# Two transformer layers in one kernel: the delta rule's norms as chains of their own, the second attention on five-unit steps, the merge as a list of pairs

## The chip, the cores and the metric

The kernel runs on one core of a Trainium2 chip. The metric is device time in microseconds for one execution of the whole program. It has five engines with an instruction queue each: PE (matrix multiplications; weight loads are listed as PEld), DVE (vector), ACT (activations and copies), POOL and SP. Each queue is worked off in its written order, and an instruction that waits for a semaphore holds up everything behind it on its engine. All the tensors are float32, and a sequence of 256 tokens with 2048 channels passes through.

## The reference, cut to what matters

Two layers follow each other. The first has a projection, an indexed attention, a state-space part and an MLP. The second is this:

```python
def hybrid_layer_2(x, ...):
    h = rms_norm(x, ln1_w)
    nsa_q, nsa_kv, nsa_gate, gdn_qkv, gdn_z, gdn_a, gdn_b, merge = split(h @ w_in)
    o_a = nsa_attention(nsa_q, nsa_kv, nsa_gate, rel_table, ...)      # 8 heads, three branches
    o_b = gated_deltanet(gdn_qkv, gdn_z, gdn_a, gdn_b, ...)           # 8 heads
    g_a, g_b = split(sigmoid(merge))
    x = x + (g_a * (o_a @ w_pa) + g_b * (o_b @ w_pb)) @ w_o
    h = rms_norm(x, ln2_w)
    return x + square(relu(h @ w_up)) @ w_down

def gated_deltanet(...):
    qkv = silu(causal_depthwise_conv(qkv, conv_w))
    q, k, v = split(qkv)
    q = q * rsqrt(sum(q * q) + eps) * 128 ** -0.5                     # norm of q
    k = k * rsqrt(sum(k * k) + eps)                                   # norm of k
    o = chunked delta rule(q, k, v, g, beta)                          # chunks of 64 tokens
    o = o * rsqrt(mean(o * o) + eps) * norm_w                         # norm of the output
    return o * silu(z)
```

The relative bias of `nsa_attention` comes from a table of 32 buckets for 8 heads, spread over 512 distances. The first layer's indexed attention scores each of 256 keys for two blocks of 128 queries; the first block may look at the first 128 keys alone.

## The kernel before, in words

**Weights.** Every weight matrix streams through a ring of four 1 MB pieces. A piece is two *units* of 128x1024. ACT copies a unit, rounded, to `w_hi` (L1778), DVE puts the rest in `w_lo` (L1049), and PE multiplies a unit in 16 instructions, eight with `w_hi` and 512 columns and eight with `w_lo` and 256 columns (L450, L453). Four units can be ready ahead of PE. Results leave the three GEMM banks in halves: ACT lifts one half (L1784), and DVE adds the other (L1069).

**Rounds.** The order on each engine is written by generators. `drain(a, b, c)` takes one step of each in turn until all are done; such a turn is a *round* here. In the last place stands the generator of the projections, which gives one weight unit a round; the ones before it are chains of small work which PE, DVE and ACT hand to each other, put between units so that their waits are covered. The same rounds are written for each engine.

**The second layer's stages around the change**, in units: `gdn0` and `gz0` (32, first half of the delta rule's projections) run beside the attention, two chains `nsa(0)` and `nsa(1)` of eight iterations that are four rounds long, both chains in the same round. In an iteration PE makes the logits (L875), DVE and ACT the softmax (L1586 to L1597, L2214), PE turns the probabilities (L883), ACT and DVE copy them (L2219, L1600), PE multiplies them with the values (L896). Then come the 32 units of `gdn1` and `gz1` and the 48 of `merge(0)` (gates and projections of `w_pa`), beside the delta rule: two chains, one after another for the heads' two halves, with 42 rounds a half. Six of the 86 rounds hold no unit. A half begins with the norms of q and k, in four rounds: ACT squares (L2245), PE sums with a matrix of ones (L917), ACT takes the root (L2248), DVE the reciprocal and the product (L1629, L1631); then follow decays and products of keys (L927 to L936), a matrix inverse in five levels for each of two token blocks (L942, L950, L955; DVE L1661 to L1667) and four chunks. It ends with the norm of the output (PE L1005, ACT L2280, DVE L1706 to L1715), whose result, multiplied with silu(z), is what `w_pb` is multiplied with. Then follow the 48 units of `merge(1)` alone, and `w_o`, whose input needs the merged sum converted in two parts, eight pairs on ACT (L2326) and on DVE (L1747).

**First layer.** Beside the projections of q, k and v, PE makes the bias table with eight matmuls of one head each (L571) and the sixteen score matmuls of 512 columns (L584: two heads by 256 keys).

A merge step of the kernel before is a fixed sequence of six units, gate first:

```python
for s in range(KD // 2):
    gate, proj = gate_bufs[m][s % len(gate_bufs[m])], pair(merged, s) if m == 0 else proj_bufs[s % 2]
    for i in range(6):        # units 0 to 3: two gate tiles; 4 and 5: two tiles of w_pa or w_pb
```

## Time and profile before

| what | us |
|---|---|
| time, median of 3 runs (2809.63 to 2811.53) | 2811.52 |
| time of the profiled execution | 2812.39 |
| its span, first to last instruction | 2810.4 |
| PE busy in it | 2713.7 |
| DVE busy | 1824.5 |
| ACT busy | 1375.7 |

A busy PE is one with a matmul under way. The profile lists how long each engine was busy, what its idle time waited for, and which share of TensorE's clock was granted: 1.00 is 2.4 GHz and 0.50 is 1.2 GHz. The span and what lies around it differ by 2.0 us, so what is saved in the span is saved in the time.

### The profile page before, as it was taken

To read this page: it belongs to the slowest core of one execution; us is meant where nothing else is said; L and a number is where in the kernel's file an instruction comes from. 1 tells how busy PE (TensorE), PEld (TensorE's weight loads), DVE (VectorE), ACT (ScalarE), POOL (GpSimd) and SP (SyncE) were. 2 spreads that over 40 slices of the span, in tenths; PEclk is the share of its full clock that TensorE was granted. 3 is DMA by queue.
4 is the path that set the end of the run, shared out by engine and by line. 5 is a ranking of instruction groups with operands and counts; after the bars stand their busy time and mean duration, and the time that the engine had idled before them with its cause. 6 is when DMAs were issued, how large, how long until landed. Compare 5 with 4: busy or idle time off the path is not lost. (4 is left out here: it accounts for less than half of the span.)

```text
span 2810.4 us, 38297 instructions
## 1 busy us (share of the span) xinstructions
PE 2713.7 (97%) x15590; PEld 2346.5 (83%) x15590; DVE 1824.5 (65%) x2514; ACT 1375.7 (49%) x1938; POOL 200.2 (7%) x174
## 2 busy tenths in 40 slices
PE   7999999999999999999998989999999999999998
PEld 6678888888888888888777869978888888888887
DVE  6686697655656556685658776566666556566565
ACT  5646545535445345465654444444445344454443
POOL 3004101000000000130312200000000000000001
PEclk9999999999999999999999999999999999999999
DMA  6444445555555555565333314355455555555553
GB/s 241 149 166 142 160 147 183 193 187 184 199 181 185 199 186 195 210 222 201 120 113 112 122 60 138 119 193 191 169 180 182 195 193 189 183 196 185 182 199 110
DMA packets 66711, 482.07 MB, mean 172 GB/s; under 512 B 7431, under 2 KB 7559, under 8 KB 9576
## 3 DMA queue, kind: packets, MB, share of 16 engines
q1 hardware_dynamic: 65232, 468.74, 47.9%
q0 software_dynamic: 928, 9.70, 0.9%
q8 instruction: 124, 2.03, 0.3%
q10 hardware_dynamic: 376, 1.17, 0.1%
q14 instruction: 51, 0.42, 0.0%
HBM read 473.30 MB, written 6.29 MB: 171 GB/s over the span
## 5 line engine op out<-in xcount | busy, mean ns | idle before, releaser
L1049 DVE TENSOR_TENSOR w_lo<-weight_ring,w_hi 128x1024 fp32r<-128x1024 f32 x886 | 1081.6, 1231 | 622.2 <-ACT w_hi L1778 614.5
L1778 ACT CAST w_hi<-weight_ring 128x1024 fp32r<-128x1024 f32 x886 | 917.7, 1048 | 658.7 <-PE bank L453 631.9
L450 PE MATMUL bank<-mix,w_hi 128*128 128x512 f32 x3840 | 1226.0, 401 | 8.5 <-DVE mix L1747 4.3
L450 PE MATMUL bank<-h,w_hi 128*128 128x512 f32 x2864 | 912.8, 400 | 9.3 <-DVE w_lo L1049 9.3
L453 PEld LDWEIGHTS bank<-mix,w_lo 128*128 128x128 f32 x3840 | 727.1, 189 | 172.5
L453 PE MATMUL bank<-mix,w_lo 128*128 128x256 f32 x3840 | 759.7, 279 | 0.0
L453 PEld LDWEIGHTS bank<-h,w_lo 128*128 128x128 f32 x2864 | 538.9, 188 | 127.4
L450 PEld LDWEIGHTS bank<-mix,w_hi 128*128 128x128 f32 x3840 | 590.8, 190 | 14.7 <-issue 7.7
L453 PE MATMUL bank<-h,w_lo 128*128 128x256 f32 x2864 | 563.8, 278 | 0.0
L450 PEld LDWEIGHTS bank<-h,w_hi 128*128 128x128 f32 x2864 | 439.2, 189 | 24.2 <-issue 22.6
L1784 ACT COPY arena<-bank 128x256 f32<-128x256 f32 x283 | 104.8, 372 | 383.5 <-PE bank L453 367.6
L1069 DVE TENSOR_TENSOR arena<-arena,bank 128x256 f32<-128x256 f32 x281 | 117.3, 419 | 147.0 <-ACT arena L1784 146.5
L2346 POOL TENSOR_TENSOR arena<-arena 128x512 f32<-128x512 f32 x30 | 47.2, 1574 | 1812.5 <-ACT arena L1846 1812.1
L1118 DVE TENSOR_TENSOR arena<-arena,bank 128x256 f32<-128x256 f32 x176 | 74.0, 421 | 68.1 <-PE bank L453 67.9
L2072 ACT ACTIVATE arena<-arena 128x512 f32<-128x512 f32 x64 | 40.5, 632 | 85.2 <-DVE arena L1415 85.2
L1121 DVE TENSOR_TENSOR arena<-arena,bank 128x256 f32<-128x256 f32 x176 | 74.2, 421 | 6.0
L1423 DVE TENSOR_TENSOR mix<-arena,mix 128x512 fp32r<-128x512 f32 x64 | 43.9, 686 | 10.8 <-ACT mix L2074 10.8
L1415 DVE SCALAR_TENSOR_TENSOR arena<-arena 128x512 f32<-128x512 f32 x64 | 44.3, 692 | 6.9 <-DVE arena L1069 0.5
L2362 POOL TENSOR_SCALAR arena<-arena,vecs 128x256 f32<-128x256 f32 x24 | 26.0, 1084 | 284.7 <-DVE arena L1069 244.7
L2363 POOL TENSOR_SCALAR arena<-arena,vecs 128x255 f32<-128x255 f32 x36 | 42.1, 1169 | 0.0
L2262 ACT COPY arena<-bank 128x256 f32<-128x256 f32 x40 | 14.6, 373 | 54.8 <-PE bank L950 53.6
L2074 ACT CAST mix<-arena 128x512 fp32r<-128x512 f32 x64 | 39.7, 620 | 2.0
(340 smaller groups left out, 1688.5 us busy)
## 6 DMA issues: line engine op xcount, KB each, us to landing
weight_ring<-in_w_up SPq DMA_DIRECT2D x128, 1024.0 KB, 4.9
weight_ring<-in_w_down SPq DMA_DIRECT2D x128, 1024.0 KB, 4.8
weight_ring<-in_w_merge SPq DMA_DIRECT2D x32, 1024.0 KB, 4.9
weight_ring<-in_w_gdn SPq DMA_DIRECT2D x24, 1024.0 KB, 4.9
weight_ring<-in_w_papb SPq DMA_DIRECT2D x16, 1024.0 KB, 4.8
weight_ring<-in_w_o SPq DMA_DIRECT2D x16, 1024.0 KB, 4.9
weight_ring<-in_w_xbc SPq DMA_DIRECT2D x12, 1024.0 KB, 4.9
weight_ring<-in_w_q SPq DMA_DIRECT2D x8, 1024.0 KB, 4.8
```

Source lines behind the costliest of these rows:

```text
L450: e.matmul(bank[:, :], w_hi[:, unit_at % UNITS, o + j * P:o + (j + 1) * P], x[:, :, at + j * S:at + (j + 1) * S], start=first and j == 0, ...
L453: done = e.matmul(bank[:, 0:S], w_lo[:, unit_at % UNITS, o + j * P:o + (j + 1) * P], x[:, 0, at + j * S:at + (j + 1) * S], start=False, st ...
L1049: e.tensor_tensor(w_lo[:, i, :], ring[:, p % PIECES, half * UNIT:(half + 1) * UNIT], w_hi[:, i, :].bitcast(F32), ALU.subtract).then_inc(un ...
L1069: e.tensor_tensor(dst, dst, bank[:, 0:S], ALU.add).then_inc(read, 1)
L1118: e.tensor_tensor(tile(xT, t), tile(xT, t), bank[:, 0:S], ALU.add).then_inc(res_half, 1)
L1121: e.tensor_tensor(tile(xT, t), tile(xT, t), bank[:, S:2 * S], ALU.add).then_inc(read, 1)
L1415: e.scalar_tensor_tensor(out=split(buf, 2), in0=split(buf, 2), scalar=0.0, in1=over(root_m, 2), op0=ALU.max, op1=ALU.mult).then_inc(up_sca ...
L1423: e.tensor_tensor(pair(hid[:, 1, :], n % 8), relu_m[n % 3], pair(hid[:, 0, :], n % 8).bitcast(F32), ALU.subtract).then_inc(up_lo, 1)
L1778: e.copy(w_hi[:, i, :], ring[:, p % PIECES, half * UNIT:(half + 1) * UNIT]).then_inc(unit_hi, 1)
L1784: e.copy(dst, psum[use % 3][0:dst.shape[0], S:2 * S]).then_inc(lifted, 1)
L2346: e.tensor_tensor(sq_total, sq_total, sq_bufs[s % 2], ALU.add).then_inc(res_gathered, 1)
L2363: e.tensor_scalar(tmp[:, 1:S], src[:, 0:S - 1], vec(name, 2 * tiles + t), None, ALU.mult).then_inc(conv_near, 1)
```

## The change

- The norms of q and k leave `delta_rule`. `unit_vectors(half)` is a chain of its own with four norms, one after another: for the first half it runs beside the attention from round 22 on, for the second beside the first half's delta rule from round 21 on. The sum goes to bank 7, square and root to free space in `h` (`h_plain`).
- The output's norm becomes `delta_out(half, c)`. For the first half it runs together with the second half's `delta_rule`, and the two chains are two rounds apart.
- `nsa` takes five rounds an iteration where it took four, and chain 1 begins two rounds after chain 0. DVE gives up its turn between the maximum and the reciprocal.
- The merge is a list of pairs of tiles, `gate` (four units) or `proj` (two). Three gates go beside the attention (12 units), 15 pairs (44 units) beside the delta rule, 14 (40 units) behind it. The six empty rounds are gone. The merged sum is converted from the pair `proj 1, 6` on, and one pair of eight is left for after the merge.
- First layer: one bias matmul of eight columns of output for all heads, written out to the same DRAM table by a broadcasting DMA; the eight score matmuls of the first query block take 256 columns and not 512.

```diff
@@ order of the merge
+MERGE_EARLY = [("gate", 0, 0), ("gate", 0, 1), ("gate", 0, 2)]
+MERGE_BEFORE = [("gate", 0, 3), ("gate", 0, 4), ("proj", 0, 0), ("proj", 0, 1), ("proj", 0, 2), ("gate", 0, 5),
...
+                ("proj", 0, 7), ("gate", 1, 0), ("gate", 1, 1)]
+MERGE_BEHIND = [item for s in range(6) for item in (("proj", 1, s), ("gate", 1, s + 2))] + [("proj", 1, 6), ("proj", 1, 7)]
@@ PE, first layer
-                for hd in range(NSA_HEADS):
-                    if hd > 0:
-                        e.wait_ge(rows_copied, hd)
-                    e.matmul(psum[7][:, :], rel[:, hd:hd + 1].to_broadcast([REL_BUCKETS + 1, P]), hot, start=True,
-                             stop=True).then_inc(rows_summed, 1)
-                    yield from rounds(2)
+                e.matmul(psum[7][0:NSA_HEADS, :], rel, hot, start=True, stop=True).then_inc(rows_summed, 1)
...
-                    e.matmul(psum[3 + n % 2][:, :], tile(qiT, t)[:, qb * P:(qb + 1) * P], kiT, start=True,
-                             stop=True).then_inc(score_dotted, 1)
+                    nk = P * (qb + 1)
+                    e.matmul(split(psum[3 + n % 2][:, :], 2)[:, :, 0:nk], tile(qiT, t)[:, qb * P:(qb + 1) * P],
+                             split(kiT, 2)[:, :, 0:nk], start=True, stop=True).then_inc(score_dotted, 1)
@@ PE, attention
+                yield from rounds(2 * c)
...
-                    yield from rounds(2)
+                    yield from rounds(3)
@@ PE, norms
+            def unit_vectors(half):
+                for n in range(4 * half, 4 * half + 4):
+                    yield
+                    e.wait_ge(unit_squared, n + 1)
...
+                    e.matmul(psum[7][:, :], ones[:, :], unit_sq[n % 2], start=True, stop=True).then_inc(unit_summed, 1)
+                    yield
...
+            def delta_out(half, c):
+                yield from rounds(2 * c + 1)
...
+                e.matmul(psum[7][:, :], ones[:, :], tail_bufs[c][0], start=True, stop=True).then_inc(tail_pe[c], 1)
+                yield
...
+            def delta_chain(c):
+                return one_after_another(delta_rule(0, c), together(delta_out(0, c), delta_rule(1, c)), delta_out(1, c))
@@ DVE, norms
+            def unit_vectors(half):
+                for n in range(4 * half, 4 * half + 4):
+                    root = unit_root[n % 2]
+                    yield from rounds(2)
+                    e.wait_ge(unit_rooted, n + 1)
+                    e.reciprocal(root, root).then_inc(unit_inv, 1)
...
@@ every engine, the two drains
-            drain(one_after_another(compressed(), together(nsa(0), nsa(1))), gdn_projections(0))
+            drain(one_after_another(compressed(), together(nsa(0), nsa(1))),
+                  one_after_another(rounds(22), unit_vectors(0)),
+                  one_after_another(gdn_projections(0), merge(MERGE_EARLY)))
...
-            drain(one_after_another(delta_rule(0, 0), delta_rule(1, 0)),
-                  one_after_another(delta_rule(0, 1), delta_rule(1, 1)),
-                  one_after_another(gdn_projections(1), rounds(6), merge(0)))
-            drain(merge(1))
+            drain(delta_chain(0), delta_chain(1), one_after_another(rounds(21), unit_vectors(1)),
+                  one_after_another(gdn_projections(1), merge(MERGE_BEFORE)))
+            drain(merge(MERGE_BEHIND))
```

How the instructions stand now at two places. The first is DVE's queue where the first half of the delta rule gives way to the second. Before: the end of chain 1's output norm (L1706 to L1715), then the first two norms of the second half (L1629, L1631) with a unit's `w_lo` (L1049) and bank halves (L1069) between them.

```order
L1706 RECIPROCAL arena<-arena 128x512
L1708 SCALAR_TENSOR_TENSOR arena<-arena,vecs 128x512
L1712 TENSOR_TENSOR arena<-arena 128x512
L1715 TENSOR_TENSOR h<-arena,h 128x512
L1049 TENSOR_TENSOR w_lo<-weight_ring,w_hi 128x1024 x2
L1069 TENSOR_TENSOR arena<-arena,bank1 128x256
L1049 TENSOR_TENSOR w_lo<-weight_ring,w_hi 128x1024
L1069 TENSOR_TENSOR arena<-arena,bank2 128x256
L1629 RECIPROCAL arena<-arena 128x512
L1631 SCALAR_TENSOR_TENSOR arena<-arena 128x512
L1629 RECIPROCAL arena<-arena 128x512
L1631 SCALAR_TENSOR_TENSOR arena<-arena 128x512
```

Now, in the second half's rounds 3 to 5: L1780 to L1775 are the level steps (L1666, L1667, L1661 before), L1826 to L1832 chain 1's output norm, L1125 and L1145 the unit's `w_lo` and bank half.

```order
L1125 TENSOR_TENSOR w_lo<-weight_ring,w_hi 128x1024
L1780 TENSOR_TENSOR arena<-arena,bank3 128x256
L1781 TENSOR_TENSOR arena<-arena,bank3 128x256
L1775 TENSOR_TENSOR arena<-arena,const_mats 128x256
L1826 RECIPROCAL arena<-arena 128x512
L1828 SCALAR_TENSOR_TENSOR arena<-arena,vecs 128x512
L1832 TENSOR_TENSOR arena<-arena 128x512
L1780 TENSOR_TENSOR arena<-arena,bank5 128x256
L1781 TENSOR_TENSOR arena<-arena,bank5 128x256
L1775 TENSOR_TENSOR arena<-arena,const_mats 128x256
L1125 TENSOR_TENSOR w_lo<-weight_ring,w_hi 128x1024
L1145 TENSOR_TENSOR arena<-arena,bank0 128x256
```

The output norm moved from before the second half into its levels, and it stands between the level steps of chain 0 and of chain 1.

The second place is ACT's queue in the attention. Before: L2214 is the softmax of both chains at once (four instructions), L1992 the convolution's silu, L2219 the copies of turned probabilities.

```order
L1784 COPY arena<-bank0 128x256
L1992 ACT_TABLE_LOAD
L1992 ACTIVATE arena<-arena 128x256
L2214 ACT_TABLE_LOAD
L2214 ACTIVATE arena<-arena 128x128 x4
L1778 CAST w_hi<-weight_ring 128x1024 x2
L1784 COPY arena<-bank1 128x256
L1992 ACT_TABLE_LOAD
L1992 ACTIVATE arena<-arena 128x256
L2219 COPY arena<-bank3 128x256
L2219 COPY arena<-bank5 128x256
```

Now the same stage: L2312 is one chain's softmax, L2089 the silu, L2317 and L2321 copies of one chain.

```order
L2089 ACT_TABLE_LOAD
L2089 ACTIVATE arena<-arena 128x256
L2321 CAST h<-bank3 128x128
L1876 CAST w_hi<-weight_ring 128x1024
L2312 ACT_TABLE_LOAD
L2312 ACTIVATE arena<-arena 128x128 x2
L2317 COPY arena<-bank6 128x256
L1876 CAST w_hi<-weight_ring 128x1024
L1882 COPY arena<-bank1 128x256
L2089 ACT_TABLE_LOAD
L2089 ACTIVATE arena<-arena 128x256
```

The chains' exponentials stand apart now, with a table load each. In the whole program ACT's queue has 66 table loads before and 89 now, 17 and 30 of them in the attention's stage.

## Rows read from the trace of the kernel before

**Rows 1.** The page, part 1: busy us (share of the span) and instructions.
```profile
PE 2713.7 (97%) x15590; PEld 2346.5 (83%) x15590; DVE 1824.5 (65%) x2514; ACT 1375.7 (49%) x1938; POOL 200.2 (7%) x174
```
**Rows 2.** Waits of PE, 1310 to 2000 us: total us, times, longest us.
```profile
PE bank L917 <- ACT arena L2245: 13.5, 4, 7.0
PE bank L883 <- DVE arena L1597: 7.7, 8, 1.4
PE bank L450 <- DVE w_lo L1049: 6.6, 1, 6.6
PE bank L935 <- DVE arena L1631: 4.8, 3, 1.9
PE bank L450 <- DVE mix L1747: 4.3, 1, 4.3
PE bank L896 <- DVE arena L1600: 3.9, 6, 0.8
PE bank L942 <- DVE arena L1655: 3.4, 2, 2.3
PE bank L896 <- ACT arena L2219: 2.7, 1, 2.7
```
**Rows 3.** Waits of PE, 1640 to 1686 us alone.
```profile
PE bank L917 <- ACT arena L2245: 11.2, 3, 7.0
PE bank L935 <- DVE arena L1631: 1.4, 1, 1.4
```
**Rows 4.** Windows: length, busy us PE, PEld, DVE, ACT, POOL; PEclk, DMA, GB/s.
```profile
1320.00:1476.00 156.00, 141.70 (x797) 119.84 (x796) 99.92 (x201) 92.01 (x185) 36.32 (x36) 0.96 0.33 113
1476.00:1508.00 32.00, 24.19 (x133) 19.91 (x132) 30.25 (x37) 14.23 (x23) 8.04 (x8) 0.95 0.19 63
1651.00:1686.00 35.00, 28.16 (x133) 21.61 (x134) 30.22 (x34) 18.67 (x28) 0.00 (x0) 0.86 0.26 91
1845.00:1850.00 5.00, 4.80 (x18) 4.17 (x19) 3.49 (x6) 4.30 (x7) 0.00 (x0) 0.65 0.92 324
1987.00:1994.00 7.00, 6.23 (x26) 5.42 (x27) 5.23 (x10) 3.08 (x5) 0.00 (x0) 0.76 0.46 152
2200.00:2240.00 40.00, 40.00 (x232) 34.89 (x231) 23.80 (x30) 15.26 (x15) 0.00 (x0) 1.00 0.54 187
```
**Rows 5.** Groups of PE, 60 to 200 us: busy us, mean ns, idle before.
```profile
L584 PE MATMUL bank<-arena 128*128 128x512 f32 x32 | 16.4, 595 | 1.4 <-DVE arena L1178 1.4
L571 PE MATMUL bank<-arena 33*128 33x512 f32 x16 | 9.0, 641 | 0.0
```
**Rows 6.** Groups of DVE, 1300 to 1880 us.
```profile
L1049 DVE TENSOR_TENSOR w_lo<-weight_ring,w_hi 128x1024 fp32r<-128x1024 f32 x130 | 158.0, 1225 | 81.8 <-ACT w_hi L1778 81.2
...
L1629 DVE RECIPROCAL arena<-arena 128x512 f32<-128x512 f32 x8 | 26.8, 3348 | 5.2 <-ACT arena L2248 5.2
...
L1667 DVE TENSOR_TENSOR arena<-arena,bank 128x256 f32<-128x256 f32 x40 | 16.5, 412 | 0.0
...
L1712 DVE TENSOR_TENSOR arena<-arena 128x512 f32<-128x512 f32 x4 | 2.8, 692 | 0.4
```
**Rows 7.** Timeline of DVE around 1572 us: start us, us.
```profile
1572.24 1.09 DVE L1301 SCALAR_TENSOR_TENSOR arena<-arena,vecs 128x254 f32<-128x254 f32 x2
```
**Rows 8.** Timeline of ACT around 1404 us: start us, us.
```profile
1404.05 0.36 ACT L1784 COPY arena<-bank 128x256 f32<-128x256 f32 x1
1404.43 1.28 ACT L1992 ACT_TABLE_LOAD   x1
1405.72 0.42 ACT L1992 ACTIVATE arena<-arena 128x256 f32<-128x256 f32 x1
```
**Rows 9.** Timeline of PE around 1571 us, delta rule's levels, without the units.
```profile
1567.45 1.16 PE L950 MATMUL bank<-arena 128*128 128x128 f32 x8 [0.64 <-DVE arena L1661]
1571.23 0.61 PE L955 MATMUL bank<-arena 128*128 128x128 f32 x4
...
1575.81 1.05 PE L950 MATMUL bank<-arena 128*128 128x128 f32 x8
```

More of the change, by code:

```diff
@@ L235, in weight_order, with merge @@
     add("w_vsvw", 2, 2)
[L236 to L242 removed]
+    def merge(items):
+        for kind, m, s in items:
+            if kind == "gate":
+                add("w_merge", KD * m + 2 * s, 2)
+            else:
+                add("w_papb", KD // 2 * m + s, 1)
+    add("w_gdn0", 0, 12)
+    add("w_gz0", 0, 4)
+    merge(MERGE_EARLY)
+    add("w_gdn1", 0, 12)
+    add("w_gz1", 0, 4)
+    merge(MERGE_BEFORE)
+    merge(MERGE_BEHIND)
     add("w_o", 0, KD)
@@ L1579, in nsa @@
                 e.wait_ge(cmp_act, 6)
+                yield from rounds(2 * c)
                 for it in range(8):
@@ L1610, in _ @@
+            drain(one_after_another(compressed(), together(nsa(0), nsa(1))),
+                  one_after_another(rounds(22), unit_vectors(0)),
+                  one_after_another(gdn_projections(0), merge(MERGE_EARLY)))
             for c in range(2):
@@ L1925, in bias_table @@
             def bias_table():
-                for hd in range(NSA_HEADS):
-                    e.wait_ge(rows_summed, hd + 1)
-                    e.copy(rows[:, 512 * hd:512 * hd + 512], psum[7][:, :]).then_inc(rows_copied, 1)
-                    yield from rounds(2)
+                yield from rounds(3)
+                e.wait_ge(rows_summed, 1)
+                e.copy(rows, psum[7][0:NSA_HEADS, :]).then_inc(rows_copied, 1)
             def scoring():
@@ L2226, in _, with merged_split, sigmoids @@
             e.wait_ge(kv_scaled, 8)
-            drain(one_after_another(compressed(), together(nsa(0), nsa(1))), gdn_projections(0))
+            def merged_split(*pairs):
+                for s in pairs:
+                    e.wait_ge(merge_gated, s + 1)
+                    e.copy(pair(h2_hi, s), pair(merged, s)).then_inc(merged_hi, 1)
+            def sigmoids(at_use, m, s):
+                gate = gate_buf(m, s)[0]
+                bank_done(e, at_use - 1)
+                bank_done(e, at_use)
+                e.activation(gate, gate, ACT.Sigmoid).then_inc(merge_sigmoid, 1)
@@ L2228, in _ @@
+            drain(one_after_another(compressed(), together(nsa(0), nsa(1))),
+                  one_after_another(rounds(22), unit_vectors(0)),
+                  one_after_another(gdn_projections(0), merge(MERGE_EARLY)))
             for c in range(2):
@@ L2317, in _ @@
-            drain(one_after_another(delta_rule(0, 0), delta_rule(1, 0)),
-                  one_after_another(delta_rule(0, 1), delta_rule(1, 1)),
-                  one_after_another(gdn_projections(1), rounds(6), merge(0)))
-            drain(merge(1))
-            split_to(unit + UNITS)
-            for s in range(KD // 2):
-                e.wait_ge(merge_gated, s + 1)
-                if s == 0:
-                    e.wait_ge(unit_used, unit)
-                e.copy(pair(h2_hi, s), pair(merged, s)).then_inc(merged_hi, 1)
+                e.wait_ge(unit_made, 8)
@@ new lines, in delta_out, with delta_chain @@
+                if half:
+                    e.wait_ge(merge_mult, 4)
+                e.wait_ge(tail_dve[c], 4 * half + 3)
+                e.copy(mix2_hi[:, at:at + 2 * S], wide).then_inc(tail_act[c], 1)
+                yield
+            def delta_chain(c):
+                return one_after_another(delta_rule(0, c), together(delta_out(0, c), delta_rule(1, c)), delta_out(1, c))
+            drain(delta_chain(0), delta_chain(1), one_after_another(rounds(21), unit_vectors(1)),
+                  one_after_another(gdn_projections(1), merge(MERGE_BEFORE)))
@@ L2327, in _ @@
+            drain(merge(MERGE_BEHIND))
+            merged_split(7)
             drain(project_gathered(2, "ln2", mix2))
```

353 lines of the change are left out of this document (200 added, 153 removed).

## The prediction

> **What bounds the kernel now.** First I read the page's busy times: PE is busy for 2713.7 us, 97% of the span, DVE 65%, ACT 49% [rows 1]. So the time is PE's work plus its idle time, and only two things can shorten it: less work on PE, or fewer of the 97 us in which it waits. A stretch of the MLP gives the pace of work that waits for nothing: 232 matmuls in 40.00 us, all of it busy, which is 14.5 units of 16 matmuls at 2.76 us [rows 4]. The change leaves that pace and the number of units alone.
>
> Second I read the waits of PE between 1310 and 2000 us, the second layer's attention, delta rule and merge. Eight kinds add up to 46.9 us [rows 2]. By place: the attention has 7.7 + 3.9 + 2.7 = 14.3 us. The first norms of q and k (L917, L935) and the matrix inverse's start (L942) come twice, at the entry and in the middle of the delta rule. The waits of 1640 to 1686 us show the middle's share: 11.2 and 1.4 us [rows 3]. The longer wait at L942, 2.3 us, is the entry's and the other 1.1 us the middle's. That makes 2.3 + 3.4 + 2.3 = 8.0 us for the entry and 13.7 us for the middle. One wait of 6.6 us stands where the delta rule ends and `merge(1)` begins, and one of 4.3 us where `w_o` waits for the first converted pair.
>
> Third I read the granted clock by windows, since an idle PE is followed by a stretch at 1.2 GHz. What the clock falls short of 1.00, times the window's length, is PE time lost while it works: attention 0.04 x 156 = 6.2 us, entry 0.05 x 32 = 1.6, middle 0.14 x 35 = 4.9, end of the delta rule 0.35 x 5 = 1.8, `w_o` 0.24 x 7 = 1.7, together 16.2 us [rows 4]. One such stretch costs about 1.7 us. The two long windows around, the delta rule's levels, have no wait to speak of.
>
> **First layer: less work.** The eight bias matmuls of 512 columns take 9.0 us, 1.12 each, two records a matmul; seven of them go, 7.9 us. The sixteen score matmuls take 16.4 us, 1.03 each; eight get half the columns, 4.1 us [rows 5]. PE has two waits of 1.4 us in this stage, so almost all of the 12.0 us lies on the path. They end where DVE picks the top 64 keys, and this later stretch is as it was. I take 11 us (bounds 7 and 12). The table's new DMA moves the same 2 MB from eight partitions. It runs beside weight loads that have four pieces of cover, and its reader comes 50 us later; I cost it at nothing. If the cover failed, a few us would be lost once.
>
> **Attention: 14.3 us of waits, 6.2 of clock.** An iteration now has five units to cover it, and one chain does each stage where both did it in the same round. ACT and DVE get half the work between PE's request and its use. In steady rounds I see no wait left. But four norms enter here. Each is a reciprocal of 3.35 us and a product of 0.69 on DVE, 4.04 us every two rounds [rows 6]. Two rounds of DVE are then: two `w_lo` 2.45, a bank half 0.41 (the size of L1667) [rows 6], two convolution steps 1.09 [rows 7], softmax work that I estimate at 2.4 us (0.8 of an iteration of seven operations, 3 us), and 4.04: 10.4 us. PE has two units, 5.5 us, 1.03 for the sum (a product of the score's size), and attention products that I estimate at 2.8 us: 9.3 us. DVE is short by 1.1 us, four times, less what it is ahead. I take 3 us of waits and one clock stretch of 1.7 (bounds: nothing, and all of 14.3 + 6.2). Gain 14.3 + 6.2 - 4.7 = 15.8 us.
>
> ACT pays 13 more table loads here, 23 in all, at 1.28 us [rows 8]: 16.7 us here, 29.5 in all. Before, ACT is busy 92.0 of the stage's 156 us [rows 4]; with ten more units and four norms (estimated at 1.4 and 1.3 us each) and the loads it is 128 us of about 185. It is busy but does not decide. If it did, the loads would be on the path in full.
>
> The Trainium skill, page "ScalarE: Activation LUTs", section "What ACT_TABLE_LOAD costs", puts a switch at 1283 ns for the load and some 1380 ns more for a drain. In this trace a copy ends at 1404.41, the load starts at 1404.43, and the activation starts at 1405.72, when the load is over [rows 8]: nothing of a drain is seen, and the measurement decides. By the page's figure the 23 loads would be 61 us of ACT, and ACT would be close to binding in the attention.
>
> **Entry of the delta rule: 8.0 and 1.6 us.** The norms are done long before. PE begins at once with sixteen products for decays and keys, some 4 us at L950's four in 1.05 [rows 9], and has two units (5.5) until L942: 9.5 us. DVE has fourteen operations of the size of L1667 there, 5.8 us, and by my estimate waits 1 us for exponentials and 1.9 for ACT's sigmoid and table load before them: 8.7 us. The two just meet; I leave 0.5 us. Gain 9.1 us.
>
> **Beside the first half: a new cost.** The second half's norms run in rounds 21 to 29, in the levels. There PE's pace is 1575.81 - 1567.45 = 8.3 us for two rounds [rows 9], 9.3 with the sum. DVE has six level steps 2.5, two `w_lo` 2.45, a bank half 0.41, two convolution steps 1.09 and the norm 4.04: 10.5 us [rows 6, 7]. It is short by 1.2 us a pair of rounds, in three pairs, since the fourth falls in the lighter chunks. I take 3.5 us and one clock stretch of 1.7, cost 5.2 us (bounds 0 and 9).
>
> **Middle: 13.7 and 4.9 us.** The six empty rounds are gone, and so are the norms. What comes new is the output's norm in DVE's queue between the level steps of chain 0 and chain 1: a reciprocal 3.35, a product near 0.7 and one of 0.69, 4.7 us [rows 6]. Behind it waits chain 1's level step, and PE waits for that. From L955 to the next L950 PE takes 1575.81 - 1571.23 = 4.6 us [rows 9]. DVE has chain 0's three steps 1.3, then 4.7, then chain 1's 1.3, 7.3 us behind PE's first product: 3 us of wait. Chain 0's norm stands before a single step and costs about 1 us. With 0.5 for L942, 4.5 us are left, and one clock stretch. Gain 18.6 - 6.2 = 12.4 us (bounds 3 and 18.6).
>
> **End of the delta rule: 6.6 and 1.8 us.** Before, both output norms stood in one round, and ACT's next unit behind them. Now they are two rounds apart, and chain 1's begins two units (5.5 us) before `proj 1, 0`, which needs it. Root, reciprocal, two products, copy and rest are about 7.5 us, estimated from 3.35 and 0.69 [rows 6]. I leave 2 us and no clock stretch. Gain 6.4 us.
>
> **`w_o`: 4.3 and 1.7 us.** The wait is for the first of eight pairs. Now seven are converted earlier, and the last has the same chain of 4.3 us, but is needed after 7/8 of a column of 5.5 us, at 4.8 us. I leave 0.5 us. Gain 5.5 us.
>
> **The sum.** 11 + 15.8 + 9.1 - 5.2 + 12.4 + 6.4 + 5.5 = 55.0 us. The profiled execution took 2812.4 us (span 2810.4 and 2.0 around it), so the change would give 2757.4; that execution lies 0.9 us above the median of the runs shown, so I say 2757 us.
>
> **Rivals.**
> 1. *Every wait goes.* For it: no stretch of the trace has DVE busy over its length at PE's pace, and four units lie ready ahead of PE. Against it: two rounds of DVE with a norm are over 10 us. The gain is 12.0 + 46.9 + 16.2 = 75 us: 2737 us.
> 2. *ACT's table loads decide.* In the attention and the delta rule ACT hands a unit's `w_hi`, the exponentials and the copies to the others. If each new load delays one that PE waits for, 29.5 us come back: 2757 + 29.5 = 2786 us. Against it: ACT is at 59% in the attention before. With the drain of the Trainium skill's section above it would be 61 us that come back and 2818 us; rows 8 speak against that.
> 3. *The norms stop PE, slower than before.* DVE works its queue in order, so at each of the twelve norms all `w_lo`, bank halves and level steps behind it wait for the chain square, sum, root (with a load), reciprocal, product: about 0.6 + 1.03 + 2.0 + 3.35 + 0.69 = 7.7 us. If PE stopped for all of it each time, 92 us would come in place of 60 saved: 2812 + 32 = 2844 us. It decides from 60 / 12 = 5 us a norm on. For it: the middle's wait of 7.0 us is of this kind. Against it: DVE's turn for a norm comes a round after the root was asked for, so only 4.04 us stand in its queue.
> 4. *The first layer gives nothing*, because the top-64 search binds there: 7 to 11 us less, 2765 us. This lies in my range.
>
> **How the numbers follow.** Forecast 0.58 (2746 to 2772), rival 1 0.13, rival 2 0.22, rival 3 0.03, rival 4 0.04. The range for 8 in 10 reaches to rivals 1 and 2 on both sides: 2741 to 2784. A measurement of this kernel can tell 0.2%, 5.6 us. Only rival 3 and mishaps that eat all of 60 us are not faster: faster 0.95, same 0.02, slower 0.03.
>
> **What would show it.** In the changed profile: PE busy down by about 12 us and 20 more for the clock's stretches; waits of PE in the second layer's middle about 11 to 14 us and not 46.9; no wait of 4 us or more there; a wait of about 3 us at the level step in the second half's round 5; DVE close to fully busy around the norms in the attention; the clock at 1.00 in the delta rule's entry and in `w_o`. The prediction is wrong if PE waits for `w_hi` or exponentials on ACT, if the norms each cost 3 us or more, or if the first layer is less than 7 us shorter.

## The result and the profile after

The changed kernel takes 2773.18 us (median of four runs, 2771.18 to 2779.34), the kernel before 2811.21 us (2809.63 to 2811.53). The ratio is 0.9869, 95% interval 0.9855 to 0.9884: 38.0 us faster, where 55 were forecast. The time lies inside the range, and 16 to 17 us of the gain are missing.

The profiled execution of the changed kernel is the slowest of the four: 2779.34 us, span 2777.4. The two spans differ by 33.0 us; the changed one's execution lies 6.2 us above its median and the other 1.2 us, and 33.0 + 6.2 - 1.2 = 38.0. So sums made from the two traces must come to 33.

The page, part 1, of the changed kernel; before it was [rows 1]:
```profile
PE 2697.0 (97%) x15576; PEld 2343.4 (84%) x15576; DVE 1818.5 (65%) x2514; ACT 1401.1 (50%) x1954; POOL 203.5 (7%) x174
```
PE is busy for 16.7 us less. The other 16.3 us are idle time that went. The 16.7 are 11.4 us of matmuls in the first layer and 5.3 us of the clock's stretches, both below; the prediction had 12 and 20.

PE's waits in the changed kernel, 1305 to 1975 us, the same stages as [rows 2] (us in total, times, longest):
```profile
PE bank L502 <- DVE h L1836: 8.7, 1, 8.7
PE bank L946 <- ACT arena L2317: 8.5, 4, 5.5
PE bank L1036 <- DVE arena L1775: 6.8, 4, 3.1
PE bank L946 <- DVE arena L1678: 1.8, 2, 1.3
PE bank L961 <- ACT h_plain L2381: 1.4, 2, 0.9
PE bank L502 <- DVE mix L1689: 0.9, 1, 0.9
PE bank L1057 <- DVE arena L1788: 0.5, 1, 0.5
```
46.9 us have become 28.6. Nothing is left of the waits for roots and inverses (L917, L935, L942 before). But L946 (in the attention, the softmax's results times the values) has 10.3 us and with L961 (a norm's sum) the attention has 11.7, against 14.3 before. L1036, the delta rule's level product, has two of some 3 us in the middle. And the first projection of the last merge waits 8.7 us where it waited 6.6.

The windows of the changed kernel over the same stages: attention, entry, middle, end of the delta rule, `w_o`, with the columns of [rows 4]:
```profile
1312.00:1488.00 176.00, 164.18 (x926) 139.55 (x925) 121.96 (x220) 121.94 (x214) 39.02 (x36) 0.96 0.35 121
1488.00:1522.00 34.00, 34.00 (x226) 30.65 (x225) 22.58 (x40) 15.83 (x28) 6.19 (x6) 1.00 0.40 144
1656.00:1692.00 36.00, 29.99 (x158) 25.36 (x157) 27.23 (x42) 20.33 (x30) 0.00 (x0) 0.86 0.26 89
1830.00:1848.00 18.00, 9.31 (x46) 7.95 (x46) 11.90 (x13) 9.42 (x12) 0.59 (x1) 0.81 0.39 139
1957.00:1968.00 11.00, 10.13 (x57) 8.65 (x57) 9.64 (x13) 5.16 (x7) 0.00 (x0) 1.00 0.60 209
```
Here are such windows of the kernel before (attention, middle, end, `w_o`), wide enough to hold each stretch at the lower clock whole:
```profile
1320.00:1496.00 176.00, 156.15 (x881) 131.52 (x880) 119.60 (x214) 99.31 (x194) 40.30 (x40) 0.96 0.31 108
1640.00:1690.00 50.00, 36.15 (x180) 28.36 (x180) 42.51 (x47) 25.88 (x40) 0.00 (x0) 0.86 0.25 86
1836.00:1852.00 16.00, 9.42 (x46) 8.02 (x45) 12.67 (x14) 9.39 (x13) 0.59 (x1) 0.79 0.41 155
1981.00:1996.00 15.00, 10.74 (x53) 9.16 (x52) 11.41 (x17) 8.94 (x15) 0.00 (x0) 0.89 0.42 141
```
The clock's loss, (1.00 - granted) times length: attention 7.0 us in both; entry 1.6 and now 0; middle 7.0 and now 5.0; end of the delta rule 3.4 in both; `w_o` 1.7 and now 0. The granted clock is printed to 0.01, so the figure for 176 us is good to some 0.9 us.

Where the longest wait comes from. ACT's timeline at the end of the delta rule in the changed kernel (start us, us):
```profile
1830.30 0.62 ACT L2449 CAST h<-arena 128x512 fp32r<-128x512 f32 x1 [2.55 <-DVE arena L1832]
1830.94 1.28 ACT L2441 ACT_TABLE_LOAD   x1
1832.23 0.69 ACT L2441 ACTIVATE arena<-bank,eps 128x512 f32<-128x512 f32 x1
```
And DVE's there:
```profile
1825.26 3.35 DVE L1826 RECIPROCAL arena<-arena 128x512 f32<-128x512 f32 x1
...
1829.50 0.69 DVE L1832 TENSOR_TENSOR arena<-arena 128x512 f32<-128x512 f32 x1
...
1833.89 1.23 DVE L1125 TENSOR_TENSOR w_lo<-weight_ring,w_hi 128x1024 fp32r<-128x1024 f32 x1 [1.64 <-ACT w_hi L1876]
1835.04 3.35 DVE L1826 RECIPROCAL arena<-arena 128x512 f32<-128x512 f32 x1
...
1841.35 0.68 DVE L1836 TENSOR_TENSOR h<-arena,h 128x512 fp32r<-128x512 f32 x1
```
PE made chain 1's sum (L1098) at 1827.01 to 1828.03. Its root stands in ACT's queue behind chain 0's copy L2449, which waits for DVE's product L1832; so the root begins at 1832.23, 4.2 us after the sum. Its reciprocal stands behind a split of weights that waits for ACT's cast, and begins at 1835.04. The lower part is done at 1842.03, 14 us after the sum, and PE has waited since 1833.6.

The attention's longest wait, 5.5 us, ends at 1441.1. The changed kernel's DVE and then ACT ahead of it:
```profile
1427.99 3.34 DVE L1723 RECIPROCAL h_plain<-h_plain 128x512 f32<-128x512 f32 x1
...
1433.11 0.68 DVE L1663 SCALAR_TENSOR_TENSOR arena<-bank,arena 128x512 f32<-128x512 f32 x1
```
```profile
1434.55 0.51 ACT L2312 ACTIVATE arena<-arena 128x256 f32<-128x256 f32 x1 [4.03 <-DVE arena L1667]
...
1435.66 1.28 ACT L2386 ACT_TABLE_LOAD   x1
1436.95 0.69 ACT L2386 ACTIVATE h_plain<-bank,eps 128x512 f32<-128x512 f32 x1
...
1438.87 1.28 ACT L2093 ACT_TABLE_LOAD   x1
...
1440.48 0.57 ACT L2317 COPY arena<-bank 128x512 f32<-128x512 f32 x1
```
The reciprocal delays the masked logits (L1663) and with them the exponentials; then the next norm's root and two table loads stand ahead of L2317, on which PE waits. Here both engines are late in series, though over the stage each is busy 122 of 176 us.

This wait is not 5.5 us in every execution. The kernel of the experiment "Chain 0's copy one round later" (copy-later for short) has the same code up to the delta rule. In its profiled execution the longest wait of the attention is 3.2 us, and the attention waits 8.9 us in all, not 11.7:
```profile
PE bank L946 <- ACT arena L2317: 6.2, 4, 3.2
```
That execution lies 0.9 us below its kernel's median. The two profiles with the 5.5 us wait and this code, the changed kernel's and the one with gates first, are of executions 6.2 and 6.6 us above theirs. So a wait in the attention that falls from 5.5 to some 3 us shows nothing by itself, and the attention's figures below go against both profiles.

In the middle, DVE has chain 0's output norm ahead of the level step that PE waits for, a wait of 3.1 us:
```profile
1663.37 3.35 DVE L1826 RECIPROCAL arena<-arena 128x512 f32<-128x512 f32 x1
...
1667.61 0.69 DVE L1832 TENSOR_TENSOR arena<-arena 128x512 f32<-128x512 f32 x1
1668.22 0.75 DVE L1775 TENSOR_TENSOR arena<-arena,const_mats 128x256 f32<-128x256 f32 x2
```

### The profile page after: what moved, and what is told of

It reads as the page before. It is cut to its first block and busy times, and to the rows that moved or that the text cites. A ratio compares the mean times of both kernels' runs of the same rounds, so it can differ in the third digit from the quotient of the medians.

```text
span 2777.4 us, 38313 instructions
## 1 busy us (share of the span) xinstructions
PE 2697.0 (97%) x15576; PEld 2343.4 (84%) x15576; DVE 1818.5 (65%) x2514; ACT 1401.1 (50%) x1954; POOL 203.5 (7%) x174
## 5 line engine op out<-in xcount | busy, mean ns | idle before, releaser
L1125 DVE TENSOR_TENSOR w_lo<-weight_ring,w_hi 128x1024 fp32r<-128x1024 f32 x886 | 1082.6, 1231 | 626.4 <-ACT w_hi L1876 619.1
L502 PE MATMUL bank<-h,w_hi 128*128 128x512 f32 x2864 | 913.6, 400 | 11.4 <-DVE h L1836 8.7
L502 PEld LDWEIGHTS bank<-h,w_hi 128*128 128x128 f32 x2864 | 440.2, 190 | 19.1 <-issue 16.7
L1882 ACT COPY arena<-bank 128x256 f32<-128x256 f32 x275 | 102.0, 372 | 379.1 <-PE bank L505 362.7
L1145 DVE TENSOR_TENSOR arena<-arena,bank 128x256 f32<-128x256 f32 x273 | 113.7, 418 | 142.2 <-ACT arena L1882 142.0
L1377 DVE SCALAR_TENSOR_TENSOR arena<-arena,vecs 128x254 f32<-128x254 f32 x72 | 37.5, 522 | 1.3
```

The lines of the kernel that those rows point to most:

```text
L502: e.matmul(bank[:, :], w_hi[:, unit_at % UNITS, o + j * P:o + (j + 1) * P], x[:, :, at + j * S:at + (j + 1) * S], start=first and j == 0, ...
L1125: e.tensor_tensor(w_lo[:, i, :], ring[:, p % PIECES, half * UNIT:(half + 1) * UNIT], w_hi[:, i, :].bitcast(F32), ALU.subtract).then_inc(un ...
L1145: e.tensor_tensor(dst, dst, bank[:, 0:S], ALU.add).then_inc(read, 1)
L1882: e.copy(dst, psum[use % 3][0:dst.shape[0], S:2 * S]).then_inc(lifted, 1)
```

## The experiments

The theory after the comparison: the missing time lies at the end of the delta rule and in the attention, where norms stand in queues of work that PE waits for. The rivals: ACT's table loads decide; or a wait that is taken away comes back elsewhere. Unless said otherwise, an experiment is the changed kernel with the edit shown, measured together with the kernel before; "less" and "more" are against the changed kernel's median of 2773.18 us. Differences of medians below 3 us are not taken as told apart.

**Gates first behind the delta rule.**
```diff
-MERGE_BEHIND = [... (("proj", 1, s), ("gate", 1, s + 2))] + ...
+MERGE_BEHIND = [... (("gate", 1, s + 2), ("proj", 1, s))] + ...
+                                elif m == 1 and s == 2:
+                                    for c in range(2):
+                                        e.wait_ge(delta_pe[c], 2 * len(DELTA["pe"]))
```
The added wait holds ACT's first copy of the gate's results back until PE has done the delta rule.

> The changed kernel with one reordering: behind the delta rule the gate (1,2) is worked before the projection (1,0), and so on in pairs, so that four units of matmuls that do not need the delta rule's normed outputs stand where TensorE waited 8.69 us (1833.70 to 1842.39) and then ran 6.83 us at half its clock. Theory (the end of the delta rule holds about 8 of the missing 17 us, because chain 1's norm is served only after chain 0's): the 8.69 us wait disappears, with it the half-clock stretch at 1838.5; time 2773 - 8.7 - 3.4 = about 2761, between 2759 and 2765. Rival (the time is set by something else, waits only move): the wait comes back before the projection or before w_o, the time stays within 3 us of 2773.


Measured 2765.41 us, ratio to before 0.9845 (0.9830 to 0.9859): 7.8 us less than the changed kernel. The wait on `h` is gone, and 2.1 us come back for `w_lo`.
The theory holds but for those 2 us (its range ended at 2765): the end of the delta rule held about 8 us.

**Norms nine rounds later in the attention.**
```diff
-                  one_after_another(rounds(22), unit_vectors(0)),
+                  one_after_another(rounds(31), unit_vectors(0)),
```


> The changed kernel with the norms of the first half's q and k begun nine rounds later in the second layer's attention (round 31 for round 22 on all three engines), where the convolutions' activations are mostly done. Theory (DVE's reciprocals of 3.35 us and ACT's roots fall into steps that are already full and hold up the copy of the turned weights, L2317): the 5.52 us wait at 1435.69 and the 10.24 us at half clock behind it (5.1 us) go, the attention's waits fall from 11.7 to about 4 us: time about 2773 - 10 = 2763, between 2761 and 2767. Rival (the norms cost the same wherever they stand): a wait of 4 to 6 us turns up in the later rounds or at the delta rule's first product, the time stays between 2770 and 2776.


Measured 2770.95 us, ratio 0.9859 (0.9844 to 0.9873), 2.2 us less: not told apart. The long wait moved to another step, 4.9 us at 1443, on DVE's copy L1678.
The rival is right: in the time it cannot be told where the norms start.

**No root.** Left out is the root of the twelve norms.
```diff
-                    e.activation(unit_root[n % 2], psum[7][:, :], ACT.Sqrt, ...)
+                    e.activation(unit_root[n % 2], psum[7][:, :], ACT.Square, ...)
```
(and the same at the output's root.)


> The changed kernel with ScalarE's square root in the twelve norms of q, k and outputs replaced by a square of the same shape; left out is the root, so the outputs are not the reference's. It takes away the load of the root's table before each, and some of the loads of the next function's table behind it: up to 24 loads of 1.28 us on ScalarE. Theory (the length of the chain counts only where it is exposed): at the end each chain's norm is 1.3 to 2.6 us shorter, so the 8.69 us wait falls by 3 to 5, the 5.52 us wait by 2.6; together with the clock 6 to 9 us: 2764 to 2767. Rival (ScalarE's table loads decide the stage): the waits of attention and of both places of the delta rule go nearly all, 18 us or more: 2755 or less.


Measured 2768.57 us, ratio 0.9854 (0.9838 to 0.9871): 4.6 us less. ACT has 70 table loads for 89, so 19 x 1.28 = 24.4 us less of them, and a fifth of that reaches the time: ACT's loads do not decide. At the end of the delta rule the wait is 6.5 us for 8.7, so there the root is a part of the chain. The attention's longest is 3.5 us for 5.5, but the copy-later kernel has 3.2 there with its roots, so nothing is shown for the attention.

**No inverse.** Left out is the reciprocal of the twelve norms; a constant stands for it.
```diff
-                    e.reciprocal(root, root).then_inc(unit_inv, 1)
+                    e.tensor_scalar(out=root, in0=root, scalar1=0.0, scalar2=0.02, op0=ALU.mult, op1=ALU.add)...
```
(and the same for the outputs.)


> The changed kernel with VectorE's reciprocal of 128x512 (3.35 us) in the twelve norms of q, k and outputs replaced by a multiply and add that gives a constant, one pass of the same shape; left out are the inverse norms, so the outputs are not the reference's. Theory (VectorE's reciprocal stands in the way of the delta rule's and the attention's small steps): the two waits in the middle (3.12 and 2.89 us at L1036) fall under 1 us together, the end's 8.69 us by twice 2.6 to about 3.4, the attention's 5.52 to about 3; 5 + 5.3 + 2.5 and some clock: 14 to 18 us, 2755 to 2759. Rival (ScalarE's queue decides, VectorE has room): less than 6 us, 2767 or more.


Measured 2749.79 us, ratio 0.9785 (0.9771 to 0.9800): 23.4 us less, more than either expected. The row of DVE and the longest waits of PE in this kernel:
```profile
L1723 DVE TENSOR_SCALAR h_plain<-h_plain 128x512 f32<-128x512 f32 x8 | 3.6, 452 | 0.0
```
```profile
PE bank L946 <- ACT arena L2317: 3.9, 3, 2.8
PE bank L502 <- DVE h L1836: 3.1, 1, 3.1
```
3.35 - 0.45 = 2.9 us less at a time took 5.6 us of waits from the end and 6.3 from the delta rule's products (L1036 and L1057). The attention waits 6.6 us, 5.1 less than in the changed profile and 2.3 less than in the copy-later one. The clock stays at 1.00 in the middle and at the end, where 5.0 and 3.4 us were lost:
```profile
1640.00:1690.00 50.00, 49.77 (x325) 44.24 (x324) 38.53 (x72) 29.36 (x48) 0.00 (x0) 1.00 0.35 125
1800.00:1840.00 40.00, 36.88 (x209) 31.68 (x208) 26.57 (x34) 24.07 (x32) 0.59 (x1) 1.00 0.58 210
```
So in the delta rule DVE's reciprocal is what exposes the norms. In the attention it is a part at most: more than half of the waits stay. Nor is the clock in the middle a sure sign of it. One norm a step (below) has its reciprocals and the same two waits of 3.1 and 2.9 us there, and loses nothing:
```profile
1640.00:1690.00 50.00, 43.98 (x289) 39.12 (x289) 37.60 (x61) 27.99 (x44) 0.00 (x0) 1.00 0.31 106
```

**Inverse norms on ACT as exp(-0.5 ln).** Nothing is left out.
```diff
-                    e.activation(unit_root[n % 2], psum[7][:, :], ACT.Sqrt, bias=eps[:, 0:1], scale=1.0)...
+                    e.activation(unit_root[n % 2], psum[7][:, :], ACT.Ln, bias=eps[:, 0:1], scale=1.0)...
+                    e.wait_ge(unit_logged, n + 1)
+                    e.activation(unit_root[n % 2], unit_root[n % 2], ACT.Exp, scale=-0.5)...
-                    e.reciprocal(root, root).then_inc(unit_inv, 1)
```
(and the same for the outputs.)


> The changed kernel, nothing left out: the twelve inverse norms of q, k and outputs are made on ScalarE alone, as exp(-0.5 ln(sum + eps)), for the root on ScalarE and VectorE's reciprocal of 3.35 us. VectorE loses 12 x 3.35 = 40 us of work, ScalarE gains a second activation of 0.69 and a second table load of 1.28 in each norm, about 24 us less the loads that the next softmax's exp no longer needs. Theory (VectorE's reciprocal is what exposed the norms; the run without it gained 23 us, the one without ScalarE's roots 5): gain of the first less the price on ScalarE, 12 to 19 us: 2754 to 2761; the two waits at L1036 in the middle go, the end's 8.69 falls to about 5, the 5.52 in attention to 3 to 5. Rival (ScalarE is as full as VectorE, work moved to it costs as much as it saves): within 4 us of 2773.


Measured 2767.77 us, ratio 0.9847 (0.9832 to 0.9862): 5.4 us less, nearer the rival. The end's wait is 4.9 us and the middle's 1.7 and 1.3, as the theory says. The attention waits 12.4 us, no less than before the edit, now most of it on ACT:
```profile
PE bank L947 <- ACT arena L2314: 5.9, 3, 4.8
...
PE bank L962 <- ACT h_plain L2378: 4.7, 2, 2.8
```
ACT's timeline there shows the price, 3.9 us in one piece ahead of the next cast of weights:
```profile
1406.14 1.28 ACT L2383 ACT_TABLE_LOAD   x1
1407.44 0.69 ACT L2383 ACTIVATE h_plain<-bank,eps 128x512 f32<-128x512 f32 x1
1408.14 1.28 ACT L2385 ACT_TABLE_LOAD   x1
1409.43 0.63 ACT L2385 ACTIVATE h_plain<-h_plain 128x512 f32<-128x512 f32 x1
```
The second load stands between the logarithm and the exponential. The Trainium skill, page "ScalarE: Activation LUTs", section "Table sets: the hidden batching unit", says that one load serves both; this program loads twice, and the measurement decides.

**Gates first and exp(-0.5 ln) together.** The two edits shown above.


> The run with the inverse norms on ScalarE as exp(-0.5 ln) and also the order of gates before projections behind the delta rule, nothing left out. Theory (independent causes add): the end's wait, some 5 us with ln and exp, goes behind four units of the gate: 4 to 7 us less than the first edit alone: 2748 to 2756. Rival (the wait moves on to a later projection): same as with ln and exp alone within 2 us.


Measured 2759.91 us, ratio 0.9821 (0.9806 to 0.9836): 13.3 us less than the changed kernel, and 7.8 and 5.4 are 13.2. The two gains add up. Against gates first alone it is 5.5 us, inside the 4 to 7 expected; the time itself lies 4 us above the range, since exp(-0.5 ln) alone gave less than was hoped.

**Four rounds a step again.**
```diff
-                yield from rounds(2 * c)
-                    yield from rounds(3)
+                    yield from rounds(2)
```
(on PE, DVE and ACT; DVE also keeps its turn between the maximum and the reciprocal.)


> The changed kernel with one part undone: the second layer's attention goes again four rounds a step, both chains in the same round; the norms stay beside it at their rounds. Theory (the slower pace took away small waits, the norms put one back): the attention's waits rise from 11.7 to 17 or more (14.3 before the change, and the norms on top), the time by 5 to 10: 2778 to 2783. Rival (the pace is worth nothing, only where the norms stand counts): within 3 us of 2773.


Measured 2790.0 us, ratio 0.9929 (0.9912 to 0.9945): 16.8 us more, beyond both. The waits are the old small ones and three of some 4 us behind the norms:
```profile
PE bank L960 <- ACT h_plain L2377: 8.2, 2, 4.2
...
PE bank L945 <- ACT arena L2313: 3.9, 1, 3.9
```
So with the norms beside the attention, the slower pace is worth 16.8 us. What the pace gives without the norms was not run, so how much of it the norms take back stays an inference.

**The first layer alone**, on the kernel before: the bias table as one matmul of eight rows with the broadcasting transfer, and the scores' columns.
```diff
-                    e.matmul(psum[7][:, :], rel[:, hd:hd + 1].to_broadcast([REL_BUCKETS + 1, P]), hot, ...)
+                e.matmul(psum[7][0:NSA_HEADS, :], rel, hot, ...)
...
-                    e.matmul(psum[3 + n % 2][:, :], tile(qiT, t)[:, qb * P:(qb + 1) * P], kiT, ...)
+                    e.matmul(split(psum[3 + n % 2][:, :], 2)[:, :, 0:nk], tile(qiT, t)[:, qb * P:(qb + 1) * P], ...)
...
-            e.dma_start(bias_rows, rows)...
+            e.dma_start(bias_spread, rows.unsqueeze(1).to_broadcast([NSA_HEADS, P, 2 * S]))...
```


> The kernel before with one part of the change alone, the first layer: the bias table as one matmul of 8 rows copied to the lines of memory by a broadcasting transfer, and the scores' matmuls over the columns that are read. Theory (it stands by itself): the gap of the two profiles at the first attention step, 8.9 us, is found again: ratio to the kernel before 0.9966 to 0.9973, 2802 to 2804. Rival (later waits eat it, as 2 us between 200 and 1232 us in the profile seem to say): 2804 to 2807.


Measured 2801.13 us, ratio 0.9967 (0.9955 to 0.9979): 9.3 us less than before, as the theory says. The two rows that answer to [rows 5]:
```profile
L583 PE MATMUL bank<-arena 128*128 128x256 f32 (+1 forms) x32 | 13.0, 487 | 2.3 <-DVE arena L1177 2.3
L571 PE MATMUL bank<-arena 33*8 33x512 f32 x2 | 1.0, 591 | 0.0
```

**Chain 0's copy one round later.**
```diff
-                yield from rounds(2)
+                yield from rounds(3 - c)
```
(in ACT's `delta_out`; DVE's chain 0 makes the lower part one round later too.)


> The changed kernel with chain 0's copy of its gated output to the upper part (and VectorE's lower part with it) one round later, in both halves, so that in ScalarE's queue chain 1's root stands ahead of chain 0's copy. Theory (chain 1's norm was late because ScalarE served it behind chain 0's copy, which waits for VectorE's product: its sum was ready at 1828.1 and its root began at 1831.0): the 8.69 us wait falls by the 2.9 us to 5.5 to 6.5, the time by 2 to 4: 2769 to 2771. Rival (VectorE's split of the weights decides when the reciprocal may begin): the wait stays between 8 and 9 us and the time within 1.5 us of 2773.


Measured 2772.87 us, ratio 0.9866 (0.9851 to 0.9880): no change that can be told, as the rival had it. The wait on `h` is 7.0 us for 8.7, between the theory's 5.5 to 6.5 and the rival's 8 to 9. ACT's root begins 1.0 us after the sum and no longer 4.2, but DVE's reciprocal only at 1827.15, behind two splits of weights and chain 0's lower part:
```profile
1822.90 0.69 ACT L2441 ACTIVATE arena<-bank,eps 128x512 f32<-128x512 f32 x1
```
```profile
1823.94 1.22 DVE L1125 TENSOR_TENSOR w_lo<-weight_ring,w_hi 128x1024 fp32r<-128x1024 f32 x1
...
1825.41 1.22 DVE L1125 TENSOR_TENSOR w_lo<-weight_ring,w_hi 128x1024 fp32r<-128x1024 f32 x1
1826.55 0.69 DVE L1836 TENSOR_TENSOR h<-arena,h 128x512 fp32r<-128x512 f32 x1
1827.15 3.35 DVE L1826 RECIPROCAL arena<-arena 128x512 f32<-128x512 f32 x1
```
Of the 3.2 us that ACT's queue cost, only 1.7 reach PE. ACT's order was a part of the lateness, DVE's queue the rest.

**One norm a step, gates first.**
```diff
-                    yield
+                    yield from rounds(1 if half else 4)
```
(at the end of each norm of the first half in `unit_vectors`, on PE and ACT; 3 rounds more on DVE.)


> The changed kernel with gates before projections behind the delta rule (a kernel with that alone took 2765.4 us) and with the four norms in the second layer's attention one to a step of five rounds (rounds 22, 27, 32, 37) for one every two rounds, so that each reciprocal stands behind chain 1's masked logits and each root where neither an exp nor a copy of turned weights follows in its round. Theory (the 5.52 us wait comes where a reciprocal before the masked logits and a root before the copy fall into one step, since periods of 2 and 5 rounds pass through every phase): that wait falls under 1.5 us, the attention's waits from 11.7 to about 6, with the 10 us at half clock gone: 8 us less than 2765: 2756 to 2759. Rival (the engines are full whatever the phase, as the run with the norms nine rounds later showed, where 4.88 us were left): 2763 to 2766.


Measured 2765.05 us, ratio 0.9836 (0.9821 to 0.9850), against 2765.41 with gates first alone: nothing gained. The rival is right. The wait of 5.5 is gone, and 1.8, 2.8, 0.8 and 1.1 us stand for it, each on DVE's copy L1678, which now stands behind the reciprocal:
```profile
PE bank L946 <- DVE arena L1678: 8.3, 6, 2.8
```

**The same (gates first, one norm a step) with exp(-0.5 ln) in all norms.** The edits shown above.


> The run with gates before projections and one norm a step, and with all twelve inverse norms made on ScalarE as exp(-0.5 ln) without VectorE's reciprocal (with gates first and two rounds a norm that took 2759.9 us). Theory (phase decides in the attention, VectorE's reciprocals in the delta rule): the attention's 4.75 us wait falls under 2, its clock stretch goes: 2751 to 2755. Rival (two table loads and two activations in one round, 3.9 us, hold up the copies whatever the phase): 2758 to 2761.


Measured 2758.16 us, ratio 0.9812 (0.9795 to 0.9828), 1.8 us under the run with two rounds a norm: not told apart, the rival again.

**The mixture.** Gates first, one norm a step with root and reciprocal in the attention, exp(-0.5 ln) in the delta rule.


> Gates before projections, one norm a step in the attention, with root and reciprocal there as in the changed kernel, and exp(-0.5 ln) on ScalarE for the second half's norms and the four output norms. Theory (in the attention ScalarE is the fuller engine, in the delta rule VectorE is): as good as the run with exp(-0.5 ln) everywhere or up to 3 us better: 2750 to 2755. Rival (in the delta rule ScalarE's loads cost what VectorE's reciprocals did): no better than the run with root and reciprocal everywhere.


Measured 2755.99 us, ratio 0.9806 (0.9791 to 0.9820). It computes all of the reference and is 17 us faster than the changed kernel, 55 us faster than the one before. The range, 2750 to 2755, is missed by 1 us. Against root and reciprocal everywhere (one norm a step, gates first) it gains 9.1 us by the medians. Their profiles differ by 7.6 us, and not all of it is the edit's. Up to the delta rule the two kernels have the same code and the same waits, yet the attention (first L946 to first L1036) takes 174.3 us in the one and 169.6 in the mixture. What differs is the granted clock, 0.97 and 1.00 (one norm a step first, the mixture second):
```profile
1312.00:1488.00 176.00, 166.43 (x939) 141.56 (x938) 123.15 (x218) 124.45 (x218) 39.08 (x36) 0.97 0.37 127
1312.00:1488.00 176.00, 166.45 (x972) 142.15 (x971) 125.91 (x224) 126.73 (x221) 38.98 (x36) 1.00 0.38 132
```
From there to the end the mixture takes 5.3 us less. So the work of the delta rule's norms is better on ACT, by some 5 us in these profiles. Against exp(-0.5 ln) everywhere it gains 2.2 us, less than can be told.

## Why the prediction was right and where it was wrong

The waits are those of the changed profile, the clock's loss from the windows above, both against 33.0 us between the two spans. Only the first layer was run alone and only the pace of the attention was undone; entry, middle and `w_o` are read from the two profiles.

- **First layer**, forecast 11: PE's first wait in the first layer's attention comes at 199.6 us for 208.6, 9.0 us earlier, and the part alone gained 9.3. The bias matmuls gave the 8 us. The scores gave 16.4 - 13.0 = 3.4 for 4.1, and three waits grew by 2.9 us together: L512 has 2.9 us in two, L633 2.3 and L610 0.5, where the first two had 1.4 each and the third none.
  "Almost all of the 12.0 us lies on the path" was too much. The new transfer did cost PE nothing while it ran, 89.5 to 138.4 us: the four pieces of `w_k` landed in 18.4 us for 4.9 (median), and PE had no wait between 100 and 150 us. But the table's only reader is issued at 1216.8 us, not 50 us later.
- **Attention**, forecast 15.8: waits 14.3 to 11.7, the clock's loss 7.0 in both, gain 2.6. This is the step that failed most, by 13 us (by 10 with the 8.9 us of waits in the copy-later profile, whose clock loses 7.0 as well). It set DVE's work of two rounds against PE's, found 1.1 us missing four times, and took 3 us of waits and one clock stretch. Over the stage DVE is busy 122 of 176 us, so throughput was not short. The timelines of the longest wait show one reciprocal of 3.35 us ahead of an operation that PE's chain needs, and a root with its loads on ACT later in the same chain. Moved by nine rounds or spread to one a step, the waits moved with the norms; without the reciprocal they fell to 6.6. Those 6.6 us do not come from reciprocals, so "in steady rounds I see no wait left" failed too. That the pace helps was right: undone beside the norms, it cost 16.8 us.
- **Entry**, forecast 9.1: 8.0 us of waits to none, clock 1.6 to none, 9.6. Right.
- **Second half's norms beside the first**, forecast a cost of 5.2: L1036 waits 0.6 us at 1568 and L1057 0.5 us at 1614, where 0.64 stood at the first before [rows 9]. The cost did not come; here the same average of DVE's work erred the other way.
- **Middle**, forecast 12.4: waits 13.7 to 6.0, clock 7.0 to 5.0, gain 9.7. The 3 us at the level step behind the output's norm came (2.9), but chain 0's norm cost 3.1 and not 1. Without the reciprocal both fall under 1 us.
- **End of the delta rule**, forecast 6.4: waits 6.6 to 8.7, clock 3.4 in both, a loss of 2.1. This step failed by 8.5 us. "About 7.5 us" from the sum to the lower part counted the operations of chain 1 alone. It is 14, since ACT serves chain 1's root behind chain 0's copy and DVE its reciprocal behind splits of weights. Four units put ahead of the projection gave back 7.8 us.
- **`w_o`**, forecast 5.5: 4.3 us to 0.9 and 1.7 of clock to none, 5.1. Right.

9.0 + 2.6 + 9.6 + 0 + 9.7 - 2.1 + 5.1 = 33.9 us, for the 33.0 measured between the spans. The steps are short of the forecast by 13.2 (attention), 8.5 (end), 2.7 (middle) and 2.0 (first layer), and 5.2 us come back from the cost that did not arise. So the total is nearer than its terms are: one term that erred the other way covers a part of the shortfall, and that is luck.

The price of a clock stretch was too small as well. "About 1.7 us" was read from windows of 5 and 7 us. In a window of 16 us the end of the delta rule loses 3.4 us before the change, where 1.8 were read. After the 5.5 us wait of the changed kernel's attention the clock is granted at 0.62 from 1441 to 1452 us, a loss of 4.2 us. And an idle PE is not followed by such a stretch each time: after waits of 3.1 and 2.9 us the clock of the kernel with one norm a step stayed at 1.00.

Of the signs named beforehand, the clock at 1.00 in the entry and in `w_o`, the 3 us at the level step and the shorter first layer came. Waits of 11 to 14 us in all (28.6), none of 4 us or more (8.7 and 5.5) and a nearly full DVE around the attention's norms (70% from 1400 to 1488 us) did not, and PE did wait for ACT's copies there.

Rival 2 is not what happened: without the roots, with 19 fewer loads (24.4 us), the time fell 4.6 us. ACT did matter in the attention once DVE's work was moved to it. Rival 3's mechanism, a norm in the queue, is the one at work, at 3 to 9 us in four places and not 7.7 in twelve. Rival 4 did not come: the first layer gave its 9 us.

Left open: why spans of the same code differ by some 6 us. The changed kernel's profile has a stretch at 1.2 GHz at 319 to 323 us that the kernels with norms later and with the copy later lack. With the same code and the same waits, 1640 to 1700 us lost 5.4 us of clock in the changed kernel (0.91), 3.6 with the copy later (0.94) and none with one norm a step (1.00). Stretches at the lower clock and waits shift each other; no run here took that apart. Also open is what the attention's remaining 6.6 us of waits wait for once the reciprocals are gone: the profile names ACT's copies L2317 for 3.9 of them.

## What to carry to other kernels

A balance of busy time over a round (one turn of all the chains) tells whether an engine is short, not whether a chain is late: list what stands between the request and the use in each engine's queue at the worst phase, and count the longest single operation in full. When two chains end near each other, follow the second through queues that the first still holds. The cheapest cure at the end of the delta rule was not to speed up or shift the chain but to put independent units in front of its reader. And compare a stretch of two profiles only after looking at a third of the same code: 3 to 5 us can be the clock's.

## What was not expected of the hardware

- VectorE's reciprocal of 128x512 takes 3.35 us, a multiply and add of that size in place 0.45 us. Taking 2.9 us from each of twelve, 35 us of an engine that is busy for 65% of the span, was worth 23.4 us by the medians.
- A logarithm and an exponential that follow each other on ScalarE were given a table load of 1.28 us each: 101 loads in the program for 89.
- The granted clock after a wait is not set by the wait alone: 3.1 and 2.9 us in the middle were followed by a loss of 5.4 us from 1640 to 1700 in one kernel and by none in another with the same code there.
- The broadcasting transfer of the bias table took 48.9 us from issue to landing, where the plain one of the same 2 MB took 7.9 us. It is issued at 89.5 us for 136.4, so it still lands 5.9 us earlier than before (138.4 for 144.3).
